# The first layer of a two-layer hybrid decoder in two token parts, with running sums of the convolution in SBUF

## What is computed

```python
def conformer_conv(h, hist, w_pw1, b_pw1, w_dw, b_dw, ln_g, ln_b, w_pw2, b_pw2):
    u = h @ w_pw1 + b_pw1
    g = u[..., :D_CONV] * jax.nn.sigmoid(u[..., D_CONV:])
    gh = jnp.concatenate([hist.astype(g.dtype), g], axis=1)
    new_hist = gh[:, -CONV_HIST:]
    c = causal_dwconv(gh, w_dw, b_dw)              # 31 taps, each channel by itself
    c = jax.nn.silu(layernorm(c, ln_g, ln_b))
    return c @ w_pw2 + b_pw2, new_hist

def swiglu(h, wg, wu, wd):
    return (jax.nn.silu(h @ wg) * (h @ wu)) @ wd   # 1024 -> 2816 -> 1024
```

## Time and profile before

| | us |
|---|---|
| median of three timed runs | 3497.72 |
| lowest, highest | 3488.77, 3501.15 |
| time of the profiled execution | 3490.01 |
| its span, from first to last instruction | 3488.1 |
| mean granted TensorE clock | 0.978 |

### The profile page before, as it was taken

How to read it: one execution, slowest core, us unless ns; L and a number is a source line. 1 busy time by engine, 2 the same in 40 slices (tenths; PEclk the granted TensorE clock), 3 DMA queues, 4 the chain that set the end, 5 groups by cost and what they waited for, 6 DMA issues and landing times.

```text
span 3488.1 us, 52341 instructions
## 1 busy us (share of the span) xinstructions
PE 3325.2 (95%) x19646; PEld 3156.8 (91%) x19646; DVE 1591.4 (46%) x2619; ACT 872.0 (25%) x1570; POOL 934.1 (27%) x733
## 2 busy tenths in 40 slices
PE   4899969999999999998999999999979999999998
PEld 3888749999999999887999999999978999999998
DVE  3299962232222322646566575575654223222234
ACT  2111042211111111433333333333333111111113
POOL 2221122321111211413333334343333221112110
PEclk8999989999999999988999999999999999999999
DMA  3001001111111111110211211211111111111111
GB/s 99 25 25 30 18 5 41 43 42 46 44 42 42 42 48 42 43 46 11 59 45 36 63 50 37 63 32 49 48 35 31 42 42 48 42 42 42 44 46 58
DMA packets 226995, 147.24 MB, mean 42 GB/s; under 512 B 7796, under 2 KB 208852, under 8 KB 226866
## 3 DMA queue, kind: packets, MB, share of 16 engines
q1 hardware_dynamic: 226757, 145.96, 14.2%
q10 hardware_dynamic: 173, 0.39, 0.1%
HBM read 131.39 MB, written 15.65 MB: 42 GB/s over the span
## 4 chain that ended last, share of the span: by engine, by line
PE 83%; issue 6%; DVE 6%; ACT 2%; POOL 1%; DMA 1%; SPq 0%; DVEq 0%; POOLq 0%; ACTq 0%
PE bank L535 69%; PE bank L525 2%; PE bank L636 2%; PE bank L875 2%; PE bank L561 1%; PE bank L880 1%; PE bank L881 1%; PE bank L912 1%; PE bank L918 1%; DVE arena L1491 1%; DVE arena L1416 1%; DVE arena L1494 1%; DMA stage<-in_cf_w_pw 1%; PE bank L986 1%; DVE bank L1426 0%
## 5 line engine op out<-in xcount | busy, mean ns | idle before, releaser
L535 PE MATMUL bank<-xhi,whi 128*128 128x368 f32 x3840 | 1282.2, 334 | 33.5 <-POOL xlo L1875 25.3
L535 PE MATMUL bank<-xlo,whi 128*128 128x368 f32 x3840 | 1271.9, 331 | 0.0
L535 PE MATMUL bank<-xhi,wlo 128*128 128x368 f32 x3840 | 1269.0, 330 | 0.0
L1869 POOL TENSOR_TENSOR wlo<-stage,whi 128x1024 fp32r<-128x1024 f32 x220 | 544.5, 2475 | 1572.0 <-ACT whi L1028 1572.0
L535 PEld LDWEIGHTS bank<-xhi,whi 128*128 128x128 f32 x3840 | 724.8, 189 | 50.2 <-issue 31.8
L535 PEld LDWEIGHTS bank<-xlo,whi 128*128 128x128 f32 x3840 | 723.8, 188 | 3.5
L535 PEld LDWEIGHTS bank<-xhi,wlo 128*128 128x128 f32 x3840 | 724.2, 189 | 0.0
L1572 DVE TENSOR_TENSOR h<-h,bank 128x368 f32<-128x368 f32 x480 | 258.1, 538 | 684.0 <-PE bank L535 684.0
L535 PE MATMUL bank<-ahi,whi 128*128 128x368 f32 x1440 | 510.2, 354 | 0.0
L535 PE MATMUL bank<-ahi,wlo 128*128 128x368 f32 x1440 | 476.6, 331 | 0.0
L535 PE MATMUL bank<-alo,whi 128*128 128x368 f32 x1440 | 476.6, 331 | 0.0
(11 more groups left out here) (214 smaller groups left out, 2988.8 us busy)
## 6 DMA issues: line engine op xcount, KB each, us to landing
stage<-in_ssd_w_in SPq DMA_DIRECT2D x48, 512.0 KB, 3.9
stage<-in_ffn_w_gate SPq DMA_DIRECT2D x44, 512.0 KB, 3.7
stage<-in_ffn_w_up SPq DMA_DIRECT2D x44, 512.0 KB, 3.7
stage<-in_ffn_w_down SPq DMA_DIRECT2D x44, 512.0 KB, 3.5
stage<-in_cf_w_pw SPq DMA_DIRECT2D x24, 512.0 KB, 3.9
arena<-in_state_ssm SPq DMA_DIRECT2D x16, 512.0 KB, 4.5
out_ss_s<-arena SPq DMA_DIRECT2D x16, 512.0 KB, 3.5
stage<-in_ssd_w_out SPq DMA_DIRECT2D x16, 512.0 KB, 3.5
```

The source lines that it names most:

```text
L535: mm = pe.matmul(bank[b][:, 0:TC], w[:, slot, w0:w0 + P], x[:, k, cs], start=n == 0, stop=n == 3 * len(offs) - 1)
L1869: pool.tensor_tensor(wlo[:, slot, :], stage[:, slot, :], whi[:, slot, :].bitcast(F32), ALU.subtract)\
```

## The change

Layer 0 is done in two token parts. Part one is chunk 0 (368 columns), part two chunks 1 and 2 (736 columns). pw1 still runs for all three chunks, tile by tile. Then:

- Convolution. PE has no taps and POOL no diagonals any more. In `conv_first` DVE does all 31 taps of chunk 0's 304 prompt columns while pw1 runs, in two alternating sums (`conv_a` and `conv_odd`). For the 64 sample columns POOL forms all 31 products of each (`products`, 8 instructions of 8 x 31 a tile), and one DVE reduction adds them. The 248 taps of part two, 736 columns each, are left over: `taps(n)` puts the next n of them into DVE's later work, into a sum kept in the columns of `xlo` that part two has not yet any use for. The gated products of all tiles are kept in SBUF.
- Order. After pw1: LayerNorm, pw2, the FFN's norm and ten turns of the FFN for chunk 0 alone, with taps of part two on DVE in between (5, 8, 8 x 2, 4, 10, 4, then 19 in each turn); before the tenth turn's down products the remaining 25. Then part two's mean and LayerNorm beside the last turn of part one, pw2 for chunks 1 and 2 (`PW2B`, in an alternating order), and the FFN for chunks 1 and 2. All weights of pw2 and of the FFN are loaded and split twice, once a part.
- Weights. Part one's pw2 and FFN, and part two's pw2, use a third slot: `stage_c` with hi and lo parts in columns of `ahi` and `alo`. Lists (`PREV`, `SPLITS`) say which unit may follow which in a slot.
- Moved issues: the history's two loads go ahead of the second tile's weights on SP, the SSD state rows' load (`conv_rows`) behind the last FFN norm, the nine output copies of the convolution tail on ACT's queue behind part one's LayerNorm. The history's transposed state rows are turned after the first up products of part two.
- The FFN loop of layer 0 runs over two chunks in part two (288 matmuls a turn); layer 1 keeps three.

```diff
+PW2B = [(0, 1)] + [x for m in range(KT - 1) for x in ((m + 1, 1), (m, 2))] + [(KT - 1, 2)]
+def slot_of(u):
+    if u < U_PW2A or u >= U_FFN0:
+        return u % 2
+    if u >= U_FFN0 - 2:
+        return 2 * (u - U_FFN0 + 2)
+    return (u - U_PW2A) % 3
...
+        conv_bc = xlo_f[:, :, TC:T]
+        prod = ahi_f[:].rearrange("p j t -> p (j t)")[:, 0:NS * CW].rearrange("p (b r t) -> p b r t", b=DB, t=CW)
...
-            def taps(m, a, nt=CT):
...
+            first_gate(0)
+            first_up(0)
+            for f in range(FP - 1):
+                first_gate(f + 1)
...
+                first_down(f)
...
+                first_up(f + 1)
+            pe.wait_ge(cen_done, KT + 2)
+            add_squares(N_LN, 1, range(KT))
+            first_down(FP - 1)
+            add_squares(N_LN, 2, range(KT))
...
+            def conv_first(m):
+
+                glu_part(m, 0)
+                dve.wait_ge(g_glu, NC * m + 1)
+                base, n = (CW + 1) * m, TC - NS
+                even, odd = conv_a[:, m, NS:TC], conv_odd
+                for t in range(CW):
+                    w = params[:, C_WDW + t * KT + m:C_WDW + t * KT + m + 1]
+                    src, acc = glu[:, m, t:t + n], odd if t % 2 else even
...
+                        dve.scalar_tensor_tensor(acc, src, w, acc, ALU.mult, ALU.add).then_inc(c_step, 1)
+                    if t == 14:
+                        glu_part(m, 1)
+                    elif t == 20:
+                        glu_part(m, 2)
+                    elif t == 27:
+                        dve.wait_ge(g_prod, m + 1)
+                        dve.tensor_reduce(conv_a[:, m, 0:NS].rearrange("p (b r) -> p b r", b=DB), prod,
+                                          mybir.AxisListType.X, ALU.add).then_inc(g_red, 1)
...
+            def taps(count):
+
+                for q in range(taken[0], min(taken[0] + count, KT * CW)):
+                    m, t = tap(q)
...
+                        dve.wait_ge(d_step, q - 1)
+                        dve.scalar_tensor_tensor(acc, src, w, acc, ALU.mult, ALU.add).then_inc(d_step, 1)
...
+            def first_up(f):
+                first_act(f, 0)
+                taps(1)
+                first_lo(f, 0)
+                taps(2)
+                first_act(f, 1)
+                taps(2)
+                first_lo(f, 1)
+
+            def first_down(f):
+                for k in range(KT):
+                    dve.wait_ge(acc_done, DONE["d", f, k])
+                    hm = h[:, k, 0:TC]
+                    dve.tensor_tensor(hm, hm, bank[2 + k % 4][:, 0:TC], ALU.add).then_inc(f_down, 1)
+                    if k % 2:
+                        taps(1)
...
+            for f in range(FP - 1):
+                taps(6 if f < FP - 2 else KT * CW)
+                if f == FP - 2:
+                    dve.wait_ge(d_step, KT * CW)
+                first_down(f)
+                if f == FP - 2:
+                    center(1)
+                    center(2)
+                else:
+                    taps(4)
+                first_up(f + 1)
...
+            def products(m):
+
+                pool.wait_ge(g_glu, NC * m + 1)
+                wait(pool, g_red, m)
+                wt = params[:, C_WDW:C_WDW + CW * KT].rearrange("p (t k) -> p k t", k=KT)[:, m:m + 1, :]
+                for t in range(DL):
+                    v = pool.tensor_tensor(prod[:, :, t, :], gsam[:, m, :, t:t + CW], wt.to_broadcast([P, DB, CW]), ALU.mult)
+                v.then_inc(g_prod, 1)
...
+            for m in range(KT):
+                products(m)
+                splits(U_PW1 + 2 * m)
+                if m == KT - 1:
+                    tails(m)
+                splits(U_PW1 + 2 * m + 1)
+                if m < KT - 1:
+                    tails(m)
```

More of the change, by code:

```diff
@@ L394, in _ @@
[L394 to L402, removed]
+            for v in range(2):
+                cols(v, v, i["cf_w_pw1"][0], v * D)
@@ L645, in _ @@
             pe.wait_ge(x_kept[0], 9)
             pe.wait_ge(x_kept[1], 9)
-            pair(N_PW1, U_PW1)
-            history()
-            pw1(1)
-            taps(0, 0)
-            with turns(pe, 1, KT // 2) as m2:
-                pw1(2 * m2)
-                taps(2 * m2 - 1, 1)
-                pw1(2 * m2 + 1)
-                taps(2 * m2, 0)
-            taps(KT - 1, 1, 2 * CT)
+            for m in range(KT):
+                pw1(m)
+                if m == 0:
+                    history()
+                if m >= 2:
+                    if m == 2:
+                        pe.wait_ge(h_kept, 4)
+                    conv_mean(0, m - 2, 6)
@@ new lines, in _, with first_gate, first_up @@
+            root_of(N_FFN0, 0)
+            hi_of(N_FFN0, 0, 0)
+            hi_of(N_FFN0, 0, 1)
+            def first_gate(f):
+                for j in range(2):
+                    act.wait_ge(acc_done, DONE["g", f, j])
+                    if f:
+                        act.wait_ge(f_act, 2 * f - 2 + j + 1)
+                    act.activation(sg_a[:, j, :], bank[j][:, 0:TC], ACT.Silu).then_inc(f_gate, 1)
+                    splits(unit_first("g", f, j))
+            def first_up(f):
+                for j in range(2):
+                    act.wait_ge(f_act, 2 * f + j + 1)
+                    act.activation(ahi[:, j, 0:TC], actv_a[j], ACT.Copy).then_inc(f_hi, 1)
+                    splits(unit_first("u", f, j))
@@ new lines, in _ @@
+            for m in range(KT):
+                conv_first(m)
+            dve.wait_ge(mu_done, 1)
+            for k in range(KT):
+                dve.tensor_tensor(conv_a[:, k, :], conv_a[:, k, :], bank[6][:, 0:TC], ALU.subtract).then_inc(cen_done, 1)
+            dve.wait_ge(acc_done, A_PW2)
+            dve.wait_ge(g_glu, NC * KT)
+            taps(5)
+            invert(N_LN, 0)
+            ln_scale(0, 0)
+            ln_scale(0, 1)
+            taps(8)
+            for m in range(KT):
+                taps(2)
+                res(m, 0, N_FFN0)
@@ L1929, in _ @@
-            with turns(pool, 1, KT // 2) as m2:
-                for a in range(2):
-                    m = 2 * m2 + a
-                    split(2 * m + 2, 0)
-                    split(2 * m + 3, 1)
-                    history(m, a)
-                    tails(m, a)
-            pool.wait_ge(tp_done, NC * (KT - 1))
-            diagonals(KT - 1, 0, CW - 2 * CT)
-            norm(N_LN)
-            for m in range(KT - 2):
-                split(U_PW2 + 2 + m, m % 2)
+            def products(m):
[5 more added lines that the diff above has]
+                v.then_inc(g_prod, 1)
@@ new lines, in _ @@
+            lo_of(N_LN, 0, 0)
+            lo_of(N_LN, 0, 1)
+            for m in range(KT):
+                splits(U_PW2A + m)
+            lo_of(N_FFN0, 0, 0)
+            lo_of(N_FFN0, 0, 1)
+            for u in range(U_FIRST, U_PW2B - 2):
+                splits(u)
+            lo_of(N_LN, 1, 0)
+            lo_of(N_LN, 1, 1)
+            splits(U_PW2B - 2)
+            splits(U_PW2B - 1)
+            lo_of(N_LN, 2, 0)
+            lo_of(N_LN, 2, 1)
+            for m in range(KT - 1):
+                splits(U_PW2B + m)
```

922 lines of the change are left out of this document (542 added, 380 removed).

## The result

The changed kernel takes 3538.61 us (median of 4 runs, 3535.01 to 3540.39) where the kernel before takes 3493.24 in the runs beside it (4 runs, 3488.00 to 3501.15): ratio 1.0127, 95% interval 1.0102 to 1.0151. It is slower by 1.3%; the forecast was slower by 0.5% (3515), so the sign was right and the size was less than half of what came. The profiled execution took 3537.79 us, its span is 3536.0.

A forecast was written before the change was run, and what follows sets the result against it. PE, busy 95%, was taken to bound the kernel, with DVE setting the pace in the new order. The terms summed to +21.7 us: 3511.7 from the profiled execution, 3519.4 from the median, stated as 3515; range 3425 to 3570.

The forecast's parts named there:

- 3 to 6: Part one after pw1: LayerNorm to 345.4, pw2 to 382.6, FFN norm to 399.2, FFN loop starting at 430.
- step 8: pw2 of part two, 75.3 us, and the FFN norm behind it, 10.4 + 2.9, ending at 910.6.
- the start: Start of pw1: sample products and a split on POOL let PE start tile 1 at 126.4, 7.8 us late.
- the norm of part one: LayerNorm of part one after pw1, with nothing beside it: 20.5 us, to 345.4.
- step 6: FFN of part one: DVE and POOL splits exclude each other, turns of 36.0 us, nine turns 754.
- The splits hide: Rival, faster: POOL splits while DVE adds from PSUM, turns of about 30 us, 3461; chance 0.18.
- PE sets the pace: Rival, faster: exclusion not general, turns of 24.3 us and pw1 tiles of 24.6, 3393; chance 0.12.
- units late: Rival: three weight slots do not keep ahead, PE waits 1.2 us at each of 74 units, 3604; chance 0.05.
- Step 2: pw1, eight tiles: DVE sets the pace at 26.0 us a tile, ending at 324.9.
- lock bites harder: Rival, slower: DVE-POOL exclusion costs more, turns of 38.5 us and pw1 tiles of 28.5, 3557; chance 0.15.
- Step 7: Last turn of part one's FFN, 28.9 us, then part two's means and norm; pw2 of part two starts at 822.
- Step 9: FFN of part two: 549.8 us with its weight feed hidden, next layer starting at 1460.4.

The follow-up runs named there:

- The run with short remainders: Changed kernel with POOL forming only 64 of 1024 columns of each weight remainder in part one's FFN from the second turn; 3436.37 us.
- The two experiments on pw1: Each against the changed kernel, in pw1: DVE forms the weight remainders, 3530.00 us; POOL forms one of eight sample products from the second tile, 3517.88 us.
- the first run on pw1: Changed kernel with DVE instead of POOL forming the two weight remainders of each pw1 tile but the last; 3530.00 us, ratio 1.0099 to the kernel before.

## Why the prediction was right and wrong, point by point

The places that the prediction gave, against the trace of the changed kernel:

| step | forecast | measured | own difference |
|---|---|---|---|
| 1 and 2: end of pw1 and its taps | 324.9 | 334.1 | +9.2 |
| 3 to 6: loop of part one starts | 430 | 439.5 | +0.3 |
| 6: nine turns end | 754 | 762.9 | -0.6 |
| 7: pw2 of part two starts | 822 | 835.5 | +4.6 |
| 8: FFN of part two starts | 907.7 | 932.2 | +11.0 |
| 9: next layer starts | 1460.4 | 1492.3 | +7.4 |

(For step 8 the first product is taken: 910.6 less the 2.9 that the step had added for clock and second half.)

Right: the start (1; PE starts tile 1 at 126.25 for 126.4), the norm of part one (20.9 us for 20.5), and step 6, the largest term: turns of 35.9 us for 36.0, last taps 28.8 for 28.9. The run with short remainders shows that this was for the reason given. "The splits hide" and "PE sets the pace" are out; so is "units late" for part one, but its mechanism, a slot that comes free too late, was there at one unit of pw2 of part two, at 4.0 us instead of 1.2, where the prediction's cover of two units doesn't hold because that unit's predecessor in the slot is the product just done.

Wrong were sizes in steps 2, 7, 8 and 9; the mechanism of step 6 held. For step 8, the sums of squares between the products of pw2 of part two (timeline of PE, changed kernel), 4.65 us from one to the next:

```profile
858.41 0.78 PE L685 MATMUL bank<-arena,mean_w 128*128 128x368 f32 x2
863.07 0.78 PE L685 MATMUL bank<-arena,mean_w 128*128 128x368 f32 x2
867.71 0.78 PE L685 MATMUL bank<-arena,mean_w 128*128 128x368 f32 x2
```

The terms that were mis-sized:

- Step 2, the tile: 27.4 us for 26.0. The reduction was right (2.21 for 2.2), and so was the sum without POOL: the 23.4 us of the tile with one product and two remainders are 18.4 + 0.57 + 4.5. A product costs DVE 0.57 us, not the 0.45 that I took between 0.3 and 0.61 (1.0 a tile), and both remainders lie wholly beside taps, 2.27 each, where I took 0.85 of 4.2 (1.0); the tail copies cost nothing instead of 0.4. The two experiments on pw1 take these prices away one at a time: the tile falls to 25.4, by just what the remainders cost, and to 23.4 in the one tile in which DVE doesn't wait for PE's 24.8. The rival "lock bites harder" had this at 28.5.
- Step 7: +4.6. Taps, late products, means and centring came out at 809.9, to a few tenths where they were forecast. The lump of 20.5 us behind them names "sums" without a size; it took 25.6. In it PE forms eight sums of squares twice: the first chunk's (812.1 to 816.8) and, between the down products and pw2, the second chunk's (the row that starts at 830.80 above). The lump is short by one of the two; which of them it counted, the prediction does not say. A sum of squares takes 0.62 us there, since the trace counts two matmuls, 0.31 apart, for each.
- Step 8: +11.0. The same 0.62 stands between the tiles of pw2, where I had 0.35: products follow each other at 4.65 us instead of 4.39, some 4 us in all. The late slot is 4.0 and the half clock behind it 2.5; the third chunk's wait 4.2 as forecast, but its slow clock 2.3 instead of 1. The norm behind pw2 itself took 10.0 us, forecast 10.4.
- Step 9: +7.4. The FFN's middle is free of waits, as forecast. At its end PE is idle for 4.7 us in the last 52 (2.6 of it one wait of a sum for DVE's addition), against 1.0 us in the last 39 of the stage before the change. With two chunks in the place of three there is less to lie beside the next norm; that is my reading of the order, and no run tests it. Of the other 3.7 us no experiment tells.

The range (3425 to 3570) held the time; the forecast's own part of it, 3495 to 3535, missed it by 3.6 us. Of the 31.9 us that the sum missed, 9.2 are pw1's tile, where products and remainders were priced too low, and 23.0 are steps 7 to 9, the joints and the stages between them. The terms from rows of a repeated pattern were right to 6%, while the passages between two stages were summed as chains with too little of the work that PE itself has in them, and with a cover for weight slots that one unit did not have.

After the Trainium skill, SBUF — State Buffer, section Who interferes with whom, a DVE instruction with two SBUF inputs and a POOL instruction that reads SBUF exclude each other, and the loser blocks for all of the other's instruction. The runs agree that taps and residues give way to POOL's remainders and products. The loss they show is somewhat less than the whole instruction: a remainder that takes POOL 2.5 to 3.0 us beside taps costs DVE 2.1 to 2.3, a product that takes it 1.0 costs 0.57.

## What to carry to other kernels

Work put on an idle engine can be paid by the busy one when both read two SBUF tiles: here moving POOL's 1024-column remainders onto the already full DVE made the kernel 47 us faster, because 1.22 us of its own work is less than 2.1 us of standing still. When a stage is cut into token parts, list for every joint which norm loses the products that lay beside it, what PE itself must do in it, and from which unit each weight slot comes free; here 23 of the 31.9 us that the sum missed lay behind the turns, and none in them. And change the joint's order only as far as the next link allows: the last square moved ahead gained 4 us of 9, since POOL's four residues stood behind it.

## What was not expected of the hardware

- A tap with a single SBUF input meets POOL as well. The first tap of a tile (tensor_scalar) takes 1.08 us beside a product and 0.47 without one, in the run where DVE forms the products itself.
- POOL can be the one that stands. Its copy of 30 columns takes 3.13 us when it starts within seven taps in a row, and ends where the reduction begins. It isn't always so: in the run with one product the same copy takes 0.45 us in seven of the eight tiles, the last time within seven taps too. What decides, no run here shows. Timelines of the first run on pw1, POOL and DVE:

```profile
187.80 3.13 POOL L2227 COPY arena<-arena 128x30 f32<-128x30 f32 x1 [9.49 <-DVE arena L1694]
...
187.66 3.20 DVE L1721 SCALAR_TENSOR_TENSOR arena<-arena,params 128x304 f32<-128x304 f32 x7
190.78 2.21 DVE L1730 TENSOR_REDUCE arena<-ahi_f 128x64 f32<-128x1984 f32 x1
```

- A product of 248 columns with a broadcast weight row takes 0.57 us on DVE, where the width law of the taps gives 0.39. No run parts the broadcast from the other differences between the two.
